# A two-layer hybrid decoder step: index projection on its own, batched key scoring, top-key rounds beside other projections, early keys and head norms in neighbouring stages

## What is computed

```python
# layer 0, differential heads: the head norm
diff = pb[:, :, 0] - lam * pb[:, :, 1]
ob = jnp.einsum('bhqk,bkhe->bqhe', diff.astype(vb.dtype), vb)
ob = rms_norm(ob, subln0) * (1.0 - LAMBDA_INIT)

# layer 1: q, k, v, qi, ki, wi = split_cols(h @ w_in1, L1_WIDTHS)
def dsa_select(qi, wi, q_pos, ki, k_pos, k_sel):
    s = jnp.einsum('bqhd,bkd->bqhk', qi, ki).astype(jnp.float32) * (IDX_DIM ** -0.5)
    score = jnp.einsum('bqhk,bqh->bqk', jax.nn.relu(s), wi.astype(jnp.float32)) * (IDX_HEADS ** -0.5)
    score = jnp.where(k_pos[None, None, :] <= q_pos[None, :, None], score, -jnp.inf)
    _, idx = lax.top_k(score, k_sel)     # 128 keys of the prompt's 512, 256 of a batch's 1032
```

## Time and profile before

| | |
|---|---|
| median of 3 runs | 2061.53 us (2057.95 to 2061.79) |
| profiled execution | 2057.84 us, its span 2055.8 us |
| granted TensorE clock, mean | 0.919 of full speed |
| TensorE busy | 1803.2 us (88% of the span) |
| VectorE busy | 930.0 us (45%) |
| ScalarE busy | 585.5 us (28%) |
| GpSimd busy | 99.0 us (5%) |
| moved by DMA | 201.57 MB, 98 GB/s on average |

### The profile page before, as it was taken

One profiled execution on the slowest core, in us unless ns is written; L12 is line 12 of the kernel. 1 busy time (PEld: TensorE's weight loads), 2 busy tenths in 40 slices (PEclk: granted clock), 3 DMA queues, 4 the chain that ended last, 5 costly groups with the idle time before them and its releaser, 6 DMA issues. The chain is left out here.

```text
span 2055.8 us, 30791 instructions
## 1 busy us (share of the span) xinstructions
PE 1803.2 (88%) x11734; PEld 1447.5 (70%) x11734; DVE 930.0 (45%) x1688; ACT 585.5 (28%) x1111; POOL 99.0 (5%) x89
## 2 busy tenths in 40 slices
PE   5998793888699999999999967687889999999999
PEld 4786562555488997899778733354447899789987
DVE  3457357454433232222245659995433422223312
ACT  3322362333323221122132331353222322112211
POOL 1312021000000000000001210000000000000000
PEclk9999897999899999999999955787889999999999
DMA  5232002999422222322214300001544232133221
GB/s 170 73 123 82 26 1 93 359 351 361 179 88 62 82 77 77 82 82 82 68 61 123 88 1 5 7 1 39 156 146 109 57 84 83 57 82 82 82 77 62
DMA packets 176380, 201.57 MB, mean 98 GB/s; under 512 B 21530, under 2 KB 130778, under 8 KB 176282
## 3 DMA queue, kind: packets, MB, share of 16 engines
q1 hardware_dynamic: 171242, 193.96, 29.6%
q10 hardware_dynamic: 4960, 6.05, 0.9%
q0 software_dynamic: 80, 0.26, 0.0%
HBM read 191.02 MB, written 9.22 MB: 97 GB/s over the span
## 5 line engine op out<-in xcount | busy, mean ns | idle before, releaser
L206 PE MATMUL ps<-feat_lo,w_hi 128*128 128x288 f32 x1408 | 418.1, 297 | 8.6 <-DVEq L1811 8.6
L208 PE MATMUL ps<-feat_hi,w_hi 128*128 128x288 f32 x1408 | 418.1, 297 | 0.0
L207 PE MATMUL ps<-feat_hi,w_lo 128*128 128x288 f32 x1408 | 417.7, 297 | 0.0
L188 DVE TENSOR_TENSOR w_lo<-w_raw,w_hi 128x2048 fp32r<-128x2048 f32 x96 | 220.1, 2293 | 386.6 <-ACT w_hi L182 386.4
L182 ACT ACTIVATE w_hi<-w_raw 128x2048 fp32r<-128x2048 f32 x96 | 183.7, 1914 | 369.3 <-PE ps L214 340.7
L206 PEld LDWEIGHTS ps<-feat_lo,w_hi 128*128 128x128 f32 x1408 | 267.3, 190 | 9.8 <-DVEq L1811 9.8
L207 PEld LDWEIGHTS ps<-feat_hi,w_lo 128*128 128x128 f32 x1408 | 267.2, 190 | 0.0
L208 PEld LDWEIGHTS ps<-feat_hi,w_hi 128*128 128x128 f32 x1408 | 267.1, 190 | 0.0
L206 PE MATMUL ps<-w_lo,feat_hi 128*128 128x512 f32 (+1 forms) x448 | 179.5, 401 | 18.4 <-DVE feat_lo L1700 9.4
L207 PE MATMUL ps<-w_hi,feat_lo 128*128 128x512 f32 (+1 forms) x448 | 175.7, 392 | 0.0
L208 PE MATMUL ps<-w_hi,feat_hi 128*128 128x512 f32 (+1 forms) x448 | 175.6, 392 | 0.0
(11 more groups left out here) (270 smaller groups left out, 2476.4 us busy)
## 6 DMA issues: line engine op xcount, KB each, us to landing
s_kslot<-in_cache_l_k_dram SPq DMA_DIRECT2D x64, 512.0 KB, 7.6
s_vslot<-in_cache_l_v_dram SPq DMA_DIRECT2D x64, 512.0 KB, 7.4
w_raw<-in_w_gate_dram SPq DMA_DIRECT2D x44, 512.0 KB, 4.0
w_raw<-in_w_up_dram SPq DMA_DIRECT2D x44, 512.0 KB, 5.2
w_raw<-in_w_in_dram SPq DMA_DIRECT2D x18, 1024.0 KB, 5.3
w_raw<-in_w_down_dram SPq DMA_DIRECT2D x16, 1024.0 KB, 5.1
s_kslot<-in_cache_l_k_dram SPq DMA_DIRECT2D x64, 128.0 KB, 2.2
s_vslot<-in_cache_l_v_dram SPq DMA_DIRECT2D x64, 128.0 KB, 2.6
```

Source lines behind the costliest of these rows:

```text
L188: dve.tensor_tensor(self.K.w_lo[:, n % 2, :], self.K.w_raw[:, n % 2, :], self.K.w_hi[:, n % 2, :].bitcast(F32), ALU.subtract).then_inc(sel ...
L206: pe.matmul(out, lhs[0], rhs[1], start=start, stop=False)
L207: pe.matmul(out, lhs[1], rhs[0], start=False, stop=False)
L208: return pe.matmul(out, lhs[0], rhs[0], start=False, stop=stop)
```

## The change

**Layer 0.** The eight key pages of batch 0 are loaded by SyncE during `a0` (`EarlyKeys`), into memory that is free then. The turned keys of this batch go into the value slot, so its values are issued only when its scores are made; batch 1's keys are then loaded whole, ahead of them. `PromptSubln` and the block `sample_subln` go. In their place, `HeadNorm` sums the squares with 16 matmuls of one column, takes the mean on VectorE and the root as a power on GpSimd, both on 128x16 numbers, spreads them with 16 transposes, and applies them with four multiplies on VectorE. For the prompt this stands inside batch 0's key turns and behind its scores; for the sample rows, inside `o0` at its second and fourth token tile.

**Layer 1.** The index part is projected in a block of its own, `pi`, and all 64 page loads go with it. `score_keys` follows: four buffers for the prompt's products; the pages of all batches are turned into a buffer each; scores are made for four batches at a time, on four strips of 32 rows; the heads are mixed with one 128x32 matrix for four batches; VectorE copies the rows straight to where they are wanted. Five of the prompt's sixteen rounds run here. Then come `kv`, `q0` and `q1` in a block that is now called `p1`, with the other rounds on VectorE (`PromptTop`): four at the start, three behind `kv`, three behind `q0`, one behind `q1`. The masks are made at the start of `a1`.

```diff
@@ project
+                    if picks is not None:
+                        picks.vector(dve, b, x)
...
@@ prompt_attention
...
+                prompt_top.masks(dve)
...
+                early_keys.load(sp)
...
+class EarlyKeys:
...
+    def load(self, sp):
+        for j in range(N_PAGES):
+            page = sp.value_load(self.K.pages[0:1, j:j + 1], min_val=0, max_val=self.cache_k.shape[0] - 1)
+            sp.dma_start(self.pages[j], self.cache_k[ds(page, 1), :, :].rearrange("a k d -> (a k) d"))\
+              .then_inc(self.k_in[j], 16)
...
+class HeadNorm:
...
+    def square(self, act):
...
+            act.activation(dst, self.views[k], ACT.Square).then_inc(self.S["squared"], 1)
+    def sum_up(self, pe):
...
+            for x in range(self.per):
+                c = k * self.per + x
+                ins = pe.matmul(self.sums[:, c:c + 1], self.squares[k][:, x * P:(x + 1) * P], self.K.c("ones")[:, 0:1],
+                                start=True, stop=True)
+        ins.then_inc(self.S["summed"], 1)
+    def mean(self, dve):
+        dve.wait_ge(self.S["summed"], 1)
+        dve.tensor_scalar(self.norm[:, 0, :], self.sums, 1.0 / P, EPS, ALU.mult, ALU.add).then_inc(self.S["mean_ok"], 1)
+    def root(self, pool):
+        pool.wait_ge(self.S["mean_ok"], 1)
+        pool.tensor_tensor(self.norm[:, 1, :], self.norm[:, 0, :], self.K.c("minus_half")[:, 0:self.n * self.per],
+                           ALU.pow).then_inc(self.S["rstd_ok"], 1)
+    def spread(self, pe):
+        pe.wait_ge(self.S["rstd_ok"], 1)
+        for k in range(self.n):
...
+            for x in range(self.per):
+                c = k * self.per + x
+                ins = pe.transpose(self.bank(k)[:, x * P:(x + 1) * P], self.norm[:, 1, c:c + 1].to_broadcast([P, P]),
+                                   self.K.c("ident"))
+            ins.then_inc(self.S["spread"], 1)
+    def apply(self, dve):
+        for k in range(self.n):
...
+            dve.wait_ge(self.S["spread"], k + 1)
+            dve.scalar_tensor_tensor(out=view, in0=view, scalar=self.K.subln_col8[:, 0:1], in1=scale,
+                                     op0=ALU.mult, op1=ALU.mult).then_inc(self.S["normed"], 1)
...
@@ sample_attention
+        subln, kt_first = None, kt
+        if early is not None:
+            kt_first = [vslot.rearrange("p j d -> p (j d)")[:, g * BANK * chunks:(g + 1) * BANK * chunks]
+                        .rearrange("p (c n) -> p c n", n=BANK) for g in range(2)]
...
+            subln = HeadNorm(K, "p_subln", [K.att[:, 4 + h, 0:SEQ] for h in range(DIFF)], squares,
+                             K.ps[:, 7, :], [K.ps[:, x, :] for x in (5, 6, 7)])
...
-                    if subln is not None and isinstance(b, int) and b == 0:
-                        sp.wait_ge(subln.S["chain"], subln.STEPS)
                     sp.wait_ge(S["weighed"], b + 1)
                     sp.dma_start(vnew[:, :], new_v(b)).then_inc(S["new_v_in"], 16)
+                    if is_first(b):
+                        sp.wait_ge(S["scored"], 4)
...
             for b in range(LAST):
                 next_ids = page_ids(b + 1)
-                load_k(b + 1, next_ids, range(early))
+                ahead = N_PAGES // 2 if chunks == KC and not is_first(b) else N_PAGES
+                load_k(b + 1, next_ids, range(ahead))
                 load_v(b, ids, range(N_PAGES))
-                load_k(b + 1, next_ids, range(early, N_PAGES))
+                load_k(b + 1, next_ids, range(ahead, N_PAGES))
...
-            turn_k(0, range(len(units)))
+            turn_k(0, range(half_units))
+            if subln is not None:
+                subln.sum_up(pe)
+            turn_k(0, range(half_units, len(units)))
             scores(0)
+            if subln is not None:
+                subln.spread(pe)
+                subln.done(pe)
...
+            keys(0, range(half_units))
+            if subln is not None:
+                subln.mean(dve)
+            keys(0, range(half_units, len(units)))
+            if subln is not None:
+                subln.apply(dve)
...
@@ add_product
+                            if heads is not None and tile == tiles[0][0][0] and i == 0:
+                                if t == 1:
+                                    heads.sum_up(pe)
+                                if t == 3:
+                                    heads.spread(pe)
...
+            if heads is not None:
+                heads.square(act)
             if split:
                 for c in range(KC):
-                    act.activation(K.feat_hi[:, c, 0:TOK], K.att[:, c, :], ACT.Copy).then_inc(hi_ok, 1)
+                    act.activation(K.feat_hi[:, c, 0:SEQ], K.att[:, c, 0:SEQ], ACT.Copy).then_inc(hi_ok, 1)
+                if heads is not None:
+                    heads.done(act)
+                act.activation(K.feat_hi[:, :, SEQ:TOK], K.att[:, :, SEQ:TOK], ACT.Copy).then_inc(hi_ok, 1)
...
+                    if heads is not None and c == KC // 2:
+                        heads.mean(dve)
...
+                    heads.apply(dve)
+                    heads.done(dve)
+                dve.wait_ge(hi_ok, KC + 1)
...
+class PromptTop:
+    ROUNDS = K_PROMPT // 8
+    WITH_SCORES = 5
...
+    def rounds(self, dve, count):
+        s = self.s
+        for _ in range(count):
+            s.wait()
+            for i, v in enumerate(self.views):
+                s.ok(dve.max(self.best[:, i, :], v))
+            s.wait()
+            for i, v in enumerate(self.views):
+                s.ok(dve.match_replace(v, self.best[:, i, :], v, TAKEN))
...
+    def vector(self, dve, b, x):
+        if b < 2 and x == NT:
+            self.rounds(dve, 3)
+        if b == 2 and x == NT:
+            self.rounds(dve, 1)
+            self.s.wait()
+    def begin_vector(self, dve):
+        self.begin(dve)
+        self.rounds(dve, self.ROUNDS - self.WITH_SCORES - 7)
+    def masks(self, dve):
...
+        dve.tensor_copy(K.mask[:, 0, 0:P], K.c("causal")).then_inc(self.mask_ok, 1)
+        for i, v in enumerate(self.views):
+            to_mask(dve, K.mask[:, i + 1, 0:(i + 2) * P], v).then_inc(self.mask_ok, 1)
...
@@ score_keys
+            sp.dma_start(K.idx_weights, K.wi[0:SAMP, PT, :]).then_inc(S["weights_out"], 16)
+            sp.wait_ge(S["weights_out"], 16)
...
+                for b in range(GROUP):
+                    for h in range(IDXH):
+                        at = 32 * b + DEC_SEQ * h
+                        sp.dma_start(wt[at:at + DEC_SEQ, :], by[b, h]).then_inc(S["weights_in"], 16)
...
+            def scores(g):
...
                 for j in range(N_PAGES):
                     lo = (j % 2) * HEAD_DIM
+                    for x in range(GROUP):
+                        b = GROUP * g + x
+                        pe.matmul(K.ps[32 * x:32 * x + 32, 6 + j % 2, j // 2 * P:(j // 2 + 1) * P],
+                                  qs[lo:lo + HEAD_DIM, b, :, :].rearrange("p h q -> p (h q)"),
+                                  kt[lo:lo + HEAD_DIM, b, j // 2, :], start=True, stop=True)
...
+            def mix_heads(g):
...
+                for dst, lo, hi in ((K.ps[0:32, 1, :], 0, BANK), (K.ps[0:32, 2, :], BANK, PAST_LEN),
+                                    (NEWO, PAST_LEN, KEYS)):
+                    ins = pe.matmul(dst, mix[:, g, :], srelu[:, lo:hi], start=True, stop=True)
+                ins.then_inc(S["s_mixed"], 1)
...
+            pe.wait_ge(kidx_pages.landed, 16 * N_PAGES * DEC_BATCH)
+            for b in range(DEC_BATCH):
+                turn(b)
+                if b == GROUP + 1:
+                    scores(0)
+            mix_heads(0)
+            scores(1)
+            mix_heads(1)
...
+            dve.wait_ge(S["p_ok"], U)
+            top.begin(dve)
+            for qt in range(1, PT):
+                at = top.prompt[:, qt - 1, qt * P:(qt + 1) * P]
+                top.s.ok(dve.tensor_tensor(at, at, K.c("causal"), ALU.add))
+            dve.wait_ge(S["weights_in"], 16 * GROUP * IDXH)
+            for g in range(2):
+                ins = dve.tensor_scalar(mix[:, g, :], K.c("idx_sel"), wt[:, g:g + 1], None, ALU.mult)
...
+            def rows(g):
+                dve.wait_ge(S["s_mixed"], g + 1)
+                now = slice(32 * g, 32 * g + 32)
+                s.ok(dve.tensor_copy(sample_top.scores[now, 0:PAST_LEN].rearrange("p (g k) -> p g k", g=2), K.ps[0:32, 1:3, :]))
+                s.ok(dve.tensor_tensor(sample_top.scores[now, PAST_LEN:KEYS], NEWO, K.c("new_mask")[0:32, :], ALU.add))
+            top.rounds(dve, 3)
+            rows(0)
+            top.rounds(dve, top.WITH_SCORES - 3)
+            rows(1)
...
@@ the step
-        sample_subln(nc, K)
-    add_product(nc, K, "o0", lambda c, t: feat_lhs(K, c, t), out0, split=True, gain=1)
+            ks, K.c("new_mask"), K.coef[:, 0:1], out0_fn, early)
+    add_product(nc, K, "o0", lambda c, t: feat_lhs(K, c, t), out0, split=True, gain=1, subln=True)
...
-            sample_top = SampleTop(nc, K, pr)
```

(25 more changed lines are left out.)

393 lines of the change are left out of this document (147 added, 246 removed).

## The result

| | before | after |
|---|---|---|
| median of the runs, us | 2061.57 (4 runs, 2057.95 to 2061.79) | **2029.82** (4 runs, 2026.86 to 2031.86) |
| profiled execution, us | 2057.84, span 2055.8 | 2028.56, span 2026.7 |
| mean granted clock | 0.919 | 0.925 |

A forecast was written before the change was run, and what follows sets the result against it. Each block was judged by what ends last: VectorE's norm in layer 0's head, VectorE in layer 1's selection. -20.8 - 5.6 + 8.1 = -18.3 on 2057.84 gives 2039.5, put at 2041 between two references; range 2029 to 2054.

The forecast's parts named there:

- the index block: Layer 1's index projection: SyncE's 64 page issues, 71.7 us plus 0.4 from 1082.5, end it at 1154.6.
- The first rival: Layer 1's index block ends with its compute near 1118, not SyncE; later stages 36 earlier, 2005 us; chance 0.10.
- the third: Rival: back-to-back page loads are issued only as fast as they land, 56 us more, 2097; chance 0.08.
- The head: Start of layer 0's sample attention: with the long norm removed, the loop starts at 354.6 instead of 375.4, -20.8 us.
- the second rival: TensorE stays at the lower clock in the head of layer 0's sample attention: about 10 later, 2051; chance 0.10.
- A close fit, costed at nothing: Layer 0's sample attention: batch 0's values, issued only after the scores, arrive barely in time and add 0 us.
- The loop's period: Sign in layer 0's sample attention: exponentials stay as far apart as before; the forecast is wrong if this moves.
- The tail: Layer 0, separate norm block gone: output product's first matmul 6.2 earlier, 0.6 given back for sums and transposes, -5.6 us.
- Layer 1: Index projection, scoring, other projections and masks together: attention starts at 1306.3 instead of 1298.2, +8.1 us.
- the late rounds: Eleven prompt rounds beside layer 1's other projections, partly covered by idle times, add 10.4 us together.
- the scoring stage: Layer 1, behind the index block: 35 us, bounds 32 and 43, ending at 1190.
- My lower bound of 2: Scoring in layer 1: a new batch's 32 narrow matmuls on four strips take 2 to 7.7 us, 3.5 taken.

The follow-up runs named there:

- experiment 1: Kernel after, with the 64 index-key pages loaded during layer 0's network instead of beside the index projection: 1988.16 us, ratio 0.966.
- late_keys: Kernel after, with batch 0's keys loaded in layer 0's sample attention again, the new head norms kept: 2038.86 us, ratio 0.990.
- experiment 3: Kernel after without the eleven prompt rounds in `p1`: 2019.56 us; kernel after with one round moved from scoring to `p1`'s start: 2026.22 us.
- delay_12: Kernel after, with twelve unused 128x256 squares on ScalarE ahead of the output product's first steps: 2032.83 us, ratio 0.988.

## Why the prediction was right or wrong

**The direction and the range held**, though the measured 2029.8 lies at the edge of the forecast's own range (2029 to 2054) and the gain is half as large again as forecast. What the forecast put first held too: the norm and not the keys ended last in the head, the loop moved as a whole, and SyncE ended the index block, which took back what the shorter selection gave. That block measured 72.1 us against 72.1. Of the misses in the ledger, two of some 4 us belong to stretches that nobody costed and have opposite signs; that they nearly cancel is luck. The first rival (pages don't end the block) fell with experiment 1, and the third (they pile up) with 1.12 us a page in the source view.

**The head, 3.7 too little.** I started the turns behind all four squares, at 326.8; they started at 324.80, since two banks are free before ScalarE's first copy is due. Units and sums took 16.5 instead of 17.4, the sums among them 3.5 (331.13 to 334.62) where I took 3 between 0 and 3.9. The remaining 0.8 lies behind them: the spreading took 3.8 for 4, and the first exponentials came 2.7 behind the next batch's turns where it had been 3.2. Of the second rival, the lower clock, a part came: the granted clock was 1.00 for the first 6.3 us of turns, and 0.63 in 334.60:339.20, behind the column sums. The Trainium skill (TensorE: Matmul & The Clock Gate, Part 4: PE-mode transpose) says transposes don't count for the clock as matmuls do. This trace doesn't settle it: the clock fell once in the head, and rose again to 1.00 by 339.2 while TensorE did transposes only. The loss was about 1 us: a unit's four turns took 0.63 at the full clock and 0.84 in between (4.21 us for twenty), for five units.

**The loop, two errors of opposite sign.** "A close fit, costed at nothing" was wrong: the values of batch 0 arrive late (TensorE waits 0.78 at 361.85 for their load, and 0.64 at 363.12) and the first step is 1.4 longer, 1.8 by the step of `late_keys`. "The loop's period" does move, by 0.46 in five steps, and in the forecast that would have meant that I was wrong: the forecast doesn't name the removed `Sqrt`, whose effect lies in the loop and not where it stands. The seven table loads were in the trace of before.

**The tail, 0.9 too little.** `o0`'s first matmul came 1.8 us behind the first square (527.74, ScalarE), where I had 2.0. The two sums and two transposes, for which I took back 0.6, lie behind this first matmul, so they belong to the next row of the ledger; by the 0.243 that I named they would have been 1.0. TensorE is busy 0.50 with the sums and 0.38 with the transposes, and `o0` took 51.3 us from its first matmul to the next norm's first transpose, where it had taken 50.9.

**The network, 4.1 not foreseen**, a granted clock in two stretches that differs between kernels. No run shows that the change earned this part of the 31 us.

**Layer 1, 5.1 too much.** The index block (72.1 against 72.1), `p1` (115.8 against 114.9) and the masks (1.1) came as worked out, and the late rounds cost 10.1 in experiment 3 against my 10.4. The step that failed is the scoring stage: 29.8 us from the index block's end to kv's first matmul, not 35.7. Its granted clock was 0.79, where the selection's had been 0.52. The prompt's products took 9.5 (1118.98 to 1128.45), not 12; VectorE waited for neither mix, where I had taken 3: the row at 1140.33 shows TensorE waiting for VectorE instead, 5.45. The narrow matmuls, for which I took 3.5 between 2 and 7.7, went by in 1.16: 64 records of 18 ns each, where sixteen had taken 1.92, 120 each (the profile has two records for each of these matmuls). Before and after:

```profile
1223.30:1225.30 2.00, 1.97 (x19) 1.67 (x19) 0.29 (x1) 0.00 (x0) 0.00 (x0) 0.50 0.00 0
1129.40:1130.60 1.20, 1.20 (x74) 1.12 (x74) 1.20 (x4) 0.74 (x2) 0.00 (x0) 1.00 0.00 0
```

My lower bound of 2 let four strips go at once, but at the granted clock of 0.50 that the row of before has; here it was 1.00. At that clock four strips at once would be half of 1.92, an estimate of 0.96, so the strips overlapped almost fully. What the bound had wrong is the clock.

**Behind, 3.7 not foreseen.** From the issue of the samples' mask rows to the load of `o1`'s gain row the kernel after took 136.3 us, where it had taken 132.0, and its last batch of `s1` ran at a granted clock of 0.50 (1495.40:1512.10). The same stretch before:

```profile
1524.25:1540.95 16.70, 12.24 (x195) 6.84 (x197) 6.00 (x22) 3.72 (x13) 0.00 (x0) 0.92 0.39 117
```

In the twelve kernels that leave this part alone it took 132.0 to 137.9, also between kernels that differ only in layer 0 (`delay_12` 132.6); I can't say what sets it.

## What to carry to other kernels

A stage that is cut out into a block of its own takes its transfers along: count the issues of every queue that the barrier waits for, and put them into a block that has time for them; here that was worth 41 us, more than the change itself. Two edits at the same place can have values that depend on each other: the early keys cost 6 us with the long norm and bring 7 without it. When an instruction goes, look through the groups of the whole engine for what it caused elsewhere.

## What the hardware showed that I had not expected

- One `Sqrt` ahead of a loop of exponentials costs a table load of 1283 ns in each of seven passes, and 0.46 us of a step.
- Narrow matmuls of 32 columns that write four strips took 18 ns a record at a granted clock of 1.00, against 120 for those of one strip at 0.50.
- A network whose own work stayed the same took 427.5 to 428.0 us in eight kernels and 431.8 to 432.8 in five, with a different granted clock in two stretches; the mean clock of its first 6 us in `o0` sorts the two, and two delays ahead of it changed neither.
